# Stick-breaking scores in two fp32r passes of stacked halves, x loaded twice, and the loads before the value loop reordered

## What is computed

```python
proj = h @ w_in                       # [swa q|k|v, stick-breaking q|k|v, branch gates]
ya = swa_sink_attention(rope(qa), rope(ka), va, sinks) @ w_up_swa
yb = stick_breaking_attention(qb, kb, vb) @ w_up_sb
x = x + gate1 * ((sigmoid(ga) * ya + sigmoid(gb) * yb) @ w_out)
h2 = modulate(rmsnorm(x), shift2, scale2)
x = x + gate2 * peer(h2, ...)         # 16384 single-neuron experts, 8 heads x 16 picks per token
return rmsnorm(x, final_g)

# stick breaking, per head: 8 heads of width 64, keys strictly before the query
z = (qb @ kb.T) * 64 ** -0.5
after = sum over later keys of log_sigmoid(-z)
out = exp(log_sigmoid(z) + after) @ vb
```

## Time and profile before

| | |
|---|---|
| median of 3 runs | 1690.3 us (1689.53 to 1692.21) |
| the profiled execution | 1693.6 us, its span 1691.7 us |
| TensorE busy | 97% of the span, mean granted clock 0.993 |
| VectorE, ScalarE, GpSimd busy | 81%, 46%, 46% |
| DMA | 432 MB, 255 GB/s over the span |

### The profile page before, as it was taken

One profiled execution on the slowest core, in us unless ns is written; L12 is line 12 of the kernel. 1 busy time (PEld: TensorE's weight loads), 2 busy tenths in 40 slices (PEclk: granted clock), 3 DMA queues, 4 the chain that ended last, 5 costly groups with the idle time before them and its releaser, 6 DMA issues.

```text
span 1691.7 us, 24231 instructions
## 1 busy us (share of the span) xinstructions
PE 1639.4 (97%) x8700; PEld 1440.1 (85%) x8700; DVE 1370.9 (81%) x2691; ACT 773.5 (46%) x1327; POOL 782.3 (46%) x441
## 2 busy tenths in 40 slices
PE   6999999999999999999999899999999999999998
PEld 4687877878799999899999889999999978888886
DVE  7457656676688787999999589888879999888887
ACT  3356546543553444576767333333333343333334
POOL 0322222325356665666666355555545654333331
PEclk9999999999999999999999999999999999999999
DMA  8322242334043432668888999999998999999992
GB/s 338 110 100 87 105 181 89 137 124 150 27 142 121 151 129 97 209 235 350 329 334 339 357 390 374 343 367 353 348 363 322 347 400 398 398 367 376 379 357 98
DMA packets 141676, 432.17 MB, mean 255 GB/s; under 512 B 13584, under 2 KB 58640, under 8 KB 135696
## 3 DMA queue, kind: packets, MB, share of 16 engines
q1 hardware_dynamic: 88592, 265.61, 42.6%
q0 software_dynamic: 41472, 151.01, 23.8%
q10 hardware_dynamic: 11520, 14.42, 2.3%
HBM read 389.31 MB, written 41.68 MB: 255 GB/s over the span
## 4 chain that ended last, share of the span: by engine, by line
PE 66%; DVE 25%; DMA 4%; issue 3%; POOL 1%; ACT 1%; SPq 0%; DVEq 0%; ACTq 0%
PE bank L990 29%; PE bank L934 11%; PE bank L709 10%; PE bank L873 4%; DVE rows L1625 4%; DVE hot_j L1751 3%; DVE hot_i L1743 3%; DMA u_raw<-euT 2%; DVE hot_j L1746 2%; PE bank L735 1%; DVE arena L1703 1%; PE bank L796 1%; DVE slots L1636 1%; DVE arena L1661 1%; DVE arena L1653 1%
## 5 line engine op out<-in xcount | busy, mean ns | idle before, releaser
L934 PE MATMUL bank<-h_split,u_split 128*128 128x352 f32 x3072 | 518.3, 325 | 8.8 <-DVE u_split L1619 7.1
L934 PEld LDWEIGHTS bank<-h_split,u_split 128*128 128x128 f32 x3072 | 496.6, 189 | 16.7 <-DVE u_split L1619 8.2
L990 PE MATMUL bank<-v_late,a_late 128*128 128x512 f32 x1440 | 326.7, 389 | 1.6 <-DVE a_late L1797 1.6
L990 PEld LDWEIGHTS bank<-v_late,a_late 128*128 128x128 f32 x1440 | 270.2, 188 | 57.9 <-issue 1.8
L609 POOL DMA_INDIRECT rows<-ev,idx x128 | 175.5, 1371 | 220.8 <-DVE row_sum L1734 194.7
L582 POOL TENSOR_TENSOR block_split<-arena,block_split 128x1024 fp32r<-128x1024 f32 x48 | 118.1, 2465 | 304.7 <-ACT block_split L1054 304.7
L609 POOL DMA_INDIRECT rows<-eu,idx x128 | 187.6, 1466 | 149.6 <-DVE dots L1625 125.1
L592 POOL TENSOR_TENSOR u_split<-u_raw,u_split 128x1024 fp32r<-128x1024 f32 x72 | 173.8, 2417 | 169.7 <-ACT u_split L1199 169.5
L990 PE MATMUL bank<-v_split,a_split 128*128 128x512 f32 x864 | 205.4, 392 | 2.2 <-DVE a_split L1797 2.2
L990 PEld LDWEIGHTS bank<-v_split,a_split 128*128 128x128 f32 x864 | 162.1, 189 | 33.1 <-issue 2.5
L1734 DVE SCALAR_TENSOR_TENSOR row_sum<-rows,agate,row_sum 128x1024 f32<-128x1024 f32 x127 | 162.7, 1281 | 5.7 <-DMA rows<-ev,idx 1.6
(11 more groups left out here) (283 smaller groups left out, 2521.5 us busy)
## 6 DMA issues: line engine op xcount, KB each, us to landing
u_raw<-euT SPq DMA_DIRECT2D x128, 512.0 KB, 8.4
v_raw<-ev SPq DMA_DIRECT2D x128, 512.0 KB, 7.2
arena<-w_blocks SPq DMA_DIRECT2D x50, 512.0 KB, 9.2
arena<-w_ada SPq DMA_DIRECT2D x12, 2048.0 KB, 8.4
gates_scratch<-stage SPq DMA_DIRECT2D x24, 1024.0 KB, 13.6
gates<-gates_scratch SPq DMA_DIRECT2D x32, 768.0 KB, 10.7
gelu_scratch<-gelus ACTq DMA_DIRECT2D x80, 176.0 KB, 3.7
gelus<-gelu_scratch SPq DMA_DIRECT2D x80, 176.0 KB, 9.1
```

What stands on the lines that cost most here:

```text
L934: last = pe.matmul(ps[6 + b][:, 0:TE], us[:, b, wp, k * P:(k + 1) * P], hs[:, xp, k, 0:TE], start=(k == 0 and q == 0), stop=(k == DC - 1 a ...
L990: last = pe.matmul(ps[2 * t + f][:], a[:, ap, t * P:(t + 1) * P], v[:, vp, f * 512:(f + 1) * 512], start=(first and q == 0), stop=True, sk ...
```

## The change

- Queries and keys of the stick-breaking scores are split into fp32r halves. For head a of a pair, qst[a] (query_twice) holds the high half of its 64 query rows twice, and kst[a] (key_halves) the high half of its 64 key rows in its own 64 partitions and their low half in the other 64; q_low has the low half of the queries. A score is now two fp32r matmuls, one over 128 rows (both key halves by the high queries) and one over 64 rows (high keys by low queries).
- ScalarE writes four copies of 64 rows for a qb block where it wrote two, and two for a kb block where it wrote one. VectorE makes the low halves from PSUM: query_lows and key_lows, two operations of 64 x 512 each, in heads 1, 3 and 5 and once ahead of head 0. TensorE waits for them (qb_split, kb_split), in heads_scores and in evacuated. GpSimd no longer fills qB with zeros at the start.
- These tiles lie in the place of x, which is not read between the first norm and the out blocks; x is loaded from DRAM again (2 MB) once the last head's scores are done, ahead of the w_blocks load with index UNIT0 + 4, and the first out block waits for it.
- On SyncE, v0 to v3 are loaded before the last stage is awaited, after a wait for the three stages stored from stage 0; the last stage's pieces start with the one that gates 0 to 2 read; gates 0, 1 and 2 are loaded in between the last loads of u, the first after the first piece's store, the third after the other pieces'. The gate slots change places: gates 0 take the place of hot_i, gates 1 that of hot_j, gates 2 that of stage 1. The v loads use the semaphores of the weight blocks.

```diff
-        qB = carve(2, T)
-        kB = carve(T)
+        scratch = [arena_at + 4 * (ARENA + k * T) for k in range(DC)]
+        qst = [nc.alloc_sbuf_tensor_at(f"query_twice{a}", [P, T], F32R, offset=scratch[a])[:] for a in range(2)]
+        kst = [nc.alloc_sbuf_tensor_at(f"key_halves{a}", [P, T], F32R, offset=scratch[2 + a])[:] for a in range(2)]
+        q_low = nc.alloc_sbuf_tensor_at("query_low", [P, T], F32R, offset=scratch[4])[:]
+        top[0] += 3 * T
...
-              for b, at in enumerate((arena_at + 4 * top[0], arena_at + 4 * skt_at, hot_at))]
+              for b, at in enumerate((arena_at + 4 * skt_at, hot_at, arena_at + 4 * top[0]))]
...
+            sp.wait_ge(sb_scored, 4 * HEADS)
+            sp.dma_start(x[:], xT).then_inc(x_in, 16)
             for t in range(UNIT0 + 4, len(BLOCKS)):
...
-            for n in range(2):
-                sp.wait_ge(g_out[n], 16 * PIECES * GROUPS // 32)
-            v_load(0)
-            gate_load(0)
-            v_load(1)
-            gate_load(1)
-            for i in range(2, RING):
+            LAST = GROUPS // 16 - 1
+            for k in range(6):
+                u_load(EARLY + RING + k)
+            for n in range(LAST):
+                for b in range(4):
+                    sp.wait_ge(staged[b], 4 * (n + 1) + FREE)
+                for k in range(6):
+                    if k < PIECES:
+                        gates_store(n, k, g_out[n % 2])
+                    u_load(EARLY + RING + 6 * (n + 1) + k)
+            sp.wait_ge(g_out[0], 16 * PIECES * 3)
+            for i in range(RING):
                 v_load(i)
-            gate_load(2)
+            for b in range(4):
+                sp.wait_ge(staged[b], 4 * (LAST + 1) + FREE)
+            first = STASHED // (NK // PIECES)
+            gates_store(LAST, first, g_out[0])
+            u_load(EARLY + RING + BESIDE)
+            for j in range(1, PIECES):
+                gates_store(LAST, (first + j) % PIECES, g_out[1])
+                u_load(EARLY + RING + BESIDE + j)
+            sp.wait_ge(g_out[0], 16 * (PIECES * 3 + 1))
+            for i in range(GT):
+                if i == GT - 1:
+                    sp.wait_ge(g_out[1], 16 * (PIECES * 3 - 1))
+                gate_load(i)
+                if EARLY + RING + BESIDE + PIECES + i < STASHED + RING:
+                    u_load(EARLY + RING + BESIDE + PIECES + i)
...
-                pe.wait_ge(qb_ready, i + 1)
-                pe.wait_ge(kb_ready, i + 1)
+                pe.wait_ge(qb_split, i + 1)
+                pe.wait_ge(kb_split, i + 1)
...
-                    pe.matmul(ps[bank][:, col:col + T - b * P], kB[:, b * P:(b + 1) * P], qB[:, a, b * P:T],
-                              start=col == 0, stop=False, skip_group_check=True)
+                    at = ps[bank][:, col:col + T - b * P]
+                    pe.matmul(at, kst[a][:, b * P:(b + 1) * P], qst[a][:, b * P:T], start=col == 0, stop=False, skip_group_check=True)
+                    pe.matmul(at, kst[a][a * HD:(a + 1) * HD, b * P:(b + 1) * P], q_low[a * HD:(a + 1) * HD, b * P:T],
+                              start=False, stop=False, skip_group_check=True)
...
-                    act_(qB[0:HD, 0, :], at[0:HD, :], ACT.Copy, scale=HD ** -0.5)
-                    act_(qB[HD:P, 1, :], at[HD:P, :], ACT.Copy, scale=HD ** -0.5).then_inc(qb_ready, 1)
+                    for a in range(2):
+                        for to in (a, 1 - a):
+                            last = act_(qst[a][to * HD:(to + 1) * HD, :], at[a * HD:(a + 1) * HD, :], ACT.Copy, scale=HD ** -0.5)
+                    last.then_inc(qb_ready, 1)
                 if kind == "kb":
-                    act_(kB, at[:], ACT.Copy).then_inc(kb_ready, 1)
+                    for a in range(2):
+                        last = act_(kst[a][a * HD:(a + 1) * HD, :], at[a * HD:(a + 1) * HD, :], ACT.Copy)
+                    last.then_inc(kb_ready, 1)
...
+            def query_lows(m):
+
+                ve.wait_ge(qb_ready, m + 1)
+                at = ps[BANK[AT[("qb", m)]]]
+                for a in range(2):
+                    own = slice(a * HD, (a + 1) * HD)
+                    ins = nv.scalar_tensor_tensor(q_low[own, :], at[own, :], HD ** -0.5, qst[a][own, :].bitcast(F32), ALU.mult, ALU.subtract)
+                ins.then_inc(qb_split, 1)
+
+            def key_lows(m):
+
+                ve.wait_ge(kb_ready, m + 1)
+                at = ps[BANK[AT[("kb", m)]]]
+                for a in range(2):
+                    own, other = slice(a * HD, (a + 1) * HD), slice((1 - a) * HD, (2 - a) * HD)
+                    ins = nv.tensor_tensor(kst[a][other, :], at[own, :], kst[a][own, :].bitcast(F32), ALU.subtract)
+                ins.then_inc(kb_split, 1)
...
+                    if kind == "qb":
+                        query_lows(e)
+                    if kind == "kb":
+                        key_lows(e)
```

More of the change, by code:

```diff
@@ L428, in build @@
         u_in = [sem(f"u_in{e}") for e in range(RING)]
-        v_in = [sem(f"v_in{e}") for e in range(RING)]
+        v_in = w_in
+        tiles_in = [len(range(e, len(BLOCKS), 4)) for e in range(4)]
+        qb_split, kb_split = sem("qb_split"), sem("kb_split")
         gt_in = [sem(f"gt_in{e}") for e in range(GT)]
@@ L507, in _ @@
                 u_load(c)
[L509 to L523, removed]
             def v_load(i):
@@ L541, in gelu_load, with gates_store @@
                 sp.dma_start(gel[:, i % RING, 0:TE], gelu_dram[value_chunk(i)]).then_inc(gl_in[i % RING], 16)
-            for n in range(2):
-                sp.wait_ge(g_out[n], 16 * PIECES * GROUPS // 32)
-            v_load(0)
-            gate_load(0)
-            v_load(1)
-            gate_load(1)
-            for i in range(2, RING):
-                v_load(i)
-            gate_load(2)
+            def gates_store(n, k, done):
+                i0 = k * NK // PIECES
+                sp.dma_start(gates_dram[n][:, i0:i0 + NK // PIECES, :], stages[n % 2][:, i0:i0 + NK // PIECES, :]).then_inc(done, 16)
+            LAST = GROUPS // 16 - 1
[10 more added lines that the diff above has]
+            for i in range(RING):
+                v_load(i)
+            for b in range(4):
[13 more added lines that the diff above has]
+                    u_load(EARLY + RING + BESIDE + PIECES + i)
             for e in range(RING):
@@ L575, in _ @@
         def _(pool):
-            nc.gpsimd.memset(qR, 0.0)
-            nc.gpsimd.memset(qB, 0.0).then_inc(padded, 1)
+            nc.gpsimd.memset(qR, 0.0).then_inc(padded, 1)
             def block_low(t):
@@ L692, in evacuated @@
                 elif kind == "qb":
-                    engine.wait_ge(qb_ready, m + 1)
+                    engine.wait_ge(qb_split, m + 1)
                 elif kind == "kb":
-                    engine.wait_ge(kb_ready, m + 1)
+                    engine.wait_ge(kb_split, m + 1)
                 elif kind == "v":
@@ L1336, in v_high @@
             def v_high(i):
-                sa.wait_ge(v_in[i % RING], 16 * (i // RING + 1))
+                sa.wait_ge(v_in[i % RING], 16 * (tiles_in[i % RING] + i // RING + 1))
                 if 2 <= i < NF:
@@ L1510, in _ @@
             rope(2, halves)
+            query_lows(0)
+            key_lows(0)
             for n in range(HEADS):
@@ L1596, in _ @@
                 if kind == "out":
+                    if m == 0:
+                        ve.wait_ge(x_in, 32)
                     nv.scalar_tensor_tensor(x[:, m, :], ps[m % 2][:], part(2, m), x[:, m, :], ALU.mult, ALU.add).then_inc(x_ready, 1)
```

## The result

| | before | after |
|---|---|---|
| median of 7 runs each, in the same session | 1692.21 us | 1703.15 us |
| lowest to highest | 1689.53 to 1696.13 | 1699.48 to 1712.36 |
| profiled execution, its span | 1693.6, 1691.7 | 1704.57, 1702.3 |

The ratio is 1.0072, 95% interval 1.0057 to 1.0088: slower by about 11 us. 1688.1 was forecast, in a range that ended at 1693.5.

The account below looks back on a forecast made before the run. TensorE bounds nearly every slice, VectorE the end of heads 1, 3, 5. Terms -6.6 + 4.3 + 3.4 + 0.2 - 3.5 = -2.2 us give 1688.1 us on the timed runs' scale; 8 in 10 from 1682.3 to 1693.5.

Parts of the forecast that it names:

- The scores: Stick-breaking scores on TensorE: 1.72 us a head instead of 2.55, gaining 6.6 us over eight heads, up to 9.0.
- Rival 4: Scores not cheaper: second product and weight load per key block cost what the fp32 passes did; 1694.7 us, chance 0.07.
- Rival 2: VectorE's halves and gates both slow it: three lower clocks, passage +3.7 us; 1697.0 us, chance 0.08.
- query_lows, 4.3 us: Heads 1, 3, 5: two VectorE operations ahead of rope delay head_outputs 1.43 us each, losing 4.3 us.
- The clock in these heads: Heads 1, 3, 5: gaps of 3.0 us bring the lower clock in two of three, losing 3.4 us.
- What was costed at nothing: key_lows, extra ScalarE copies, x's second load and GpSimd's queue: nothing, save perhaps 0.2 us once in the lead-in.
- The passage: Around the last stage's stores: v loads moved earlier, one stop and its lower clock gone; net 3.5 us gained.
- the hole: DMA engines at 0.62 before the last stage's stores: 3.8 us of room for v loads taking 5.2 us.
- the stops: TensorE's three passage waits for u loads: 1.44 and 2.97 us stay, the third, 2.25 us, goes with its lower clock.
- rival 1: Clock holds after the heads' 3.0 us gaps, or scores gain near 1.13 a head; 1684.7 to 1682.3 us, chance 0.32.
- the forecast's case: The summed terms hold: 2.2 us gained, 1688.1 us, own range 1685.5 to 1690.5; chance 0.38.
- The sign set down ahead: Wrong if the heads' gap doesn't grow, a new gap precedes scores, or passage gaps exceed 6.7 us; scores chain 1.7 us.

Follow-up runs that it names:

- full_rows: Changed kernel with the second score product over all 128 rows, low queries padded with zeros in the other 64; 1692.97 us, ratio to before 1.0014.
- grouped: Changed kernel with a head's four 128-row products and masks first, then its four 64-row products; 1695.45 us, ratio to before 1.0026.
- passage_only: Kernel before with only the new order of SyncE's loads and stores and the new gate slots; 1690.27 us, ratio 0.9998.
- v_early: Kernel before with only the v0 to v3 loads moved ahead of the last stage, gates still behind the last u loads; 1688.76 us, ratio 0.9989.

## Why the prediction was wrong

- **The scores, "gained" 6.6 us: the step that failed.** They cost 4.6 us, a miss of 11.2, as large as the whole measured loss. The failing step is the price by columns, "2560 x 0.46 = 1.18 us", with every weight load taken as covered. It was read from rows without a change of row count (128 rows throughout). The full-row version confirms the price per column (1.66 us measured, 1.72 worked out). What I left out is the load at each change between 128 and 64 rows: 0.18 us, eight times in a head, 1.46. I weighed the row count only for what a 64-row product streams and allowed it to be a gain.
  The Trainium skill ("TensorE: Matmul & The Clock Gate", section "LDWEIGHTS (loading the stationary operand)") was quoted for its rule that a load goes by columns. The runs agree: 0.18 us for 64 rows, 0.19 for 128. That told the load's length, not whether it is covered. The Trainium skill ("TensorE: Matmul & The Clock Gate", section "The mechanism") says a load is pulled ahead of running products when its row group doesn't conflict or when it goes to the background buffer. In full_rows all loads are ahead; at a change of row count none is. If the background buffer served there too, these loads would have been hidden; the measurement shows that they are not.
- **Rivals.** Rival 4 ("the scores are not cheaper", 0.07, 1694.7) named the right place, but its reason, that a second product and its load cost what the fp32 passes did, is refuted by full_rows: two products over 128 rows cost 1.66 us a head. Rival 2 (0.08, 1697.0) came nearest in number, but by luck: it had three lower clocks behind the gaps and a loss in the passage, and neither occurred.
- **query_lows, 4.3 us: right.** 4.5 measured, gaps of 3.19, 3.19 and 2.94 for the 3.0 forecast, and 1.77 when it stands behind rope.
- **The clock in these heads, 3.4 us for two of three: right as a count.** Two of the three gaps were followed by the lower level; in full_rows and grouped all three. The size was right too, 1.7 us each. Missed were two more stretches inside scores without a gap, 3.3 us. I had made the idle gap the only thing to look for.
  The Trainium skill ("TensorE: Matmul & The Clock Gate", section "HAM oscillation — how this bites in real kernels") warns of longer gaps only. That is contradicted in the heads, where seven of eight gaps of 2.9 to 3.2 us in the changed kernel, full_rows and grouped were followed by the lower level. The Trainium skill ("TensorE: Matmul & The Clock Gate", section "A second HAM failure mode: psum-queue depth-cycling") says that frequent short idles between groups of products are enough. The stretches inside scores fit it: 0.2 us of uncovered load eight times a head, and none of them where the loads are covered or only two a head are not.
- **What was costed at nothing: right.** About 0.1 us in the heads, behind a first score that starts up to 0.9 us earlier or later without the change too.
- **The passage, 3.5 us gained: right about the hole, wrong about the stops.** The hole is filled, as forecast. Across runs the new order is worth 0.9 us by medians, with an interval of about 1.9 gained to 1.4 lost. The term was priced on a third stop, with its lower clock, that the second profile of the kernel before does not have. That some 4 us come back here between the two profiles of the result, near the 3.5 forecast, is luck: the one of the kernel before happens to hold that stop, its lower clock and another lower clock behind the second stop. The first two stops, said to stay at 1.44 and 2.97, moved: 2.66 and 2.88 in the changed kernel, 2.29 and 0.91 in passage_only, 1.77 and 1.05 in v_early. The loads of u took 13.4 to 20.0 us to land, not the 8 to 13 forecast. What decides how the stops fall was not found out.
- **A slip in the chances.** "Faster by over 0.2%" is rival 1 and a tenth of the forecast's case, 0.32 + 0.04 = 0.36, not 0.38. Nothing hangs on it.

The sign set down ahead points at the failed term: the head's chain is 3.12 us, against "1.4 to 1.8".

## What to carry to other kernels

Before a product over 64 rows is put between products over 128 to save work, count the changes of row count: each left some 0.2 us of weight load uncovered here, and filling the other 64 rows with zeros was 11.7 us cheaper in the chain, 10.2 by the medians. If the narrow products must stay, group them: that took 2.03 us a head for 3.12. A stop that occurs in one profiled execution is no term of a sum until a second one shows it.

## What the runs showed of the hardware that I had not expected

- The weight load at a change between 128 and 64 rows is not covered by the running product, in either direction, while loads of equal rows are: 0.18 us a change, with eight changes a head as with two. The runs do not show why, nor whether two 64-row products over different halves would behave alike.
- The granted clock fell to 1.2 GHz in stretches with TensorE busy all the time by the record (263 to 267 us: 4.00 of 4.00 busy, clock 0.61), behind dense short products with uncovered loads. All three profiles of kernels with eight changes a head have such stretches in the heads (two, one and three), and none of the other nine profiles does. That ties them to the scores with many changes; that the uncovered loads themselves are the cause is an inference.
- Whether the clock falls behind one and the same gap differs between executions of one kernel: 2.33 us ahead of the up blocks had it at 0.57 in one execution and at 1.00 in another, and in ten of the twelve profiles the lower level follows; 1.77 us in the passage had 0.58 behind it, 2.88 us had 1.00. Among gaps of these sizes their length alone does not decide it.
